# A hybrid decoder step on one core: order of loads, of shared-bank uses and of the opening MLP weights

## What is computed

```python
qa, ka, va, qb, kb, vb, fa = jnp.split(rmsnorm(x, g_attn) @ w_in, _SPLITS, axis=-1)
logf = jax.nn.log_sigmoid(fa + b_f)
s = jnp.einsum('bqhd,bkhd->bhqk', qa, ka) * scale + c_q - c_k          # forgetting: c = cumsum(logf), causal
oa = softmax(s) @ va
# dilated: for (w, d) in ((128, 1), (512, 4), (2048, 16)) a softmax over every d-th key of the last w; the three merged
x = x + concat(oa, ob) @ w_o
u = relu(rmsnorm(x, g_mlp) @ w_up)
y = x + (u * u) @ w_down
```

## Time and profile before

| | us |
|---|---|
| three timed runs | 3784.39, 3796.53, 3796.73 (median 3796.53) |
| the profiled execution, its own time | 3782.47 |
| span of its instructions | 3780.8 |
| projection / forgetting / dilated / samples (windows 0:691, 691:1167, 1167:1618, 1618:2010) | 691 / 476 / 451 / 392 |
| join, MLP of group 0 / of group 1 (2010:2144, 2144:2844 / 2844:2994, 2994:3781) | 134, 700 / 150, 787 |

### The profile page before, as it was taken

One profiled execution on the slowest core, in us unless ns is written; L12 is line 12 of the kernel. 1 busy time (PEld: TensorE's weight loads), 2 busy tenths in 40 slices (PEclk: granted clock), 3 DMA queues, 4 the chain that ended last, 5 costly groups with the idle time before them and its releaser, 6 DMA issues. The chain is left out here.

```text
span 3780.8 us, 50228 instructions
## 1 busy us (share of the span) xinstructions
PE 3532.7 (93%) x18196; PEld 2750.4 (73%) x18240; DVE 1486.2 (39%) x2869; ACT 981.8 (26%) x1424; POOL 1113.3 (29%) x1034
## 2 busy tenths in 40 slices
PE   7999999799998999979997899999998899999999
PEld 7987788455554777744445688888886788888888
DVE  2223323555535656243322343343333333333333
ACT  3322222244442222222222311112113311111111
POOL 1224366576665566501231200100101200000000
PEclk9999999899998999889998999999999999999999
DMA  6555766866657565388874211111104211111111
GB/s 199 189 172 187 229 198 222 208 158 184 182 142 191 151 179 173 109 316 310 299 257 158 67 50 45 44 44 55 55 31 154 59 45 44 37 42 39 39 44 62
DMA packets 303528, 507.60 MB, mean 134 GB/s; under 512 B 48850, under 2 KB 190676, under 8 KB 297940
## 3 DMA queue, kind: packets, MB, share of 16 engines
q1 hardware_dynamic: 266356, 370.29, 32.5%
q10 hardware_dynamic: 23032, 80.04, 6.2%
q0 software_dynamic: 13952, 54.80, 4.0%
HBM read 408.18 MB, written 164.50 MB: 151 GB/s over the span
## 5 line engine op out<-in xcount | busy, mean ns | idle before, releaser
L2900 DVE TENSOR_TENSOR fin_x<-mlp_y,fin_x 128x512 f32<-128x512 f32 x544 | 350.2, 686 | 749.8 <-PE mlp_y L2943 749.8
L2860 POOL TENSOR_TENSOR mlp_u<-fox_in_squares 128x1024 f32<-128x1024 f32 (+2 forms) x80 | 131.7, 1646 | 1325.2 <-ACT fox_in_squares L2801 1325.2
L2920 PE MATMUL mlp_u<-fin_h_hi,mlp_w_hi 128*128 128x512 f32 (+2 forms) x1280 | 451.0, 352 | 21.1 <-DVE mlp_w_lo L2876 21.1
L2921 PE MATMUL mlp_u<-fin_h_lo,mlp_w_hi 128*128 128x512 f32 (+2 forms) x1280 | 451.0, 352 | 0.0
L2922 PE MATMUL mlp_u<-fin_h_hi,mlp_w_lo 128*128 128x512 f32 (+2 forms) x1280 | 450.8, 352 | 0.0
L2943 PE MATMUL mlp_y<-mlp_w_hi,mlp_u_lo 128*128 128x512 f32 x1088 | 425.0, 391 | 0.0
L674 PE MATMUL proj_z<-proj_w_lo,proj_x_hi 128*128 128x512 f32 (+1 forms) x816 | 305.6, 375 | 0.0
L673 PE MATMUL proj_z<-proj_w_hi,proj_x_hi 128*128 128x512 f32 (+1 forms) x748 | 281.6, 376 | 11.8 <-DVE proj_w_lo L518 10.7
L675 PE MATMUL proj_z<-proj_w_hi,proj_x_lo 128*128 128x512 f32 (+1 forms) x748 | 276.2, 369 | 0.0
L2920 PEld LDWEIGHTS mlp_u<-fin_h_hi,mlp_w_hi 128*128 128x128 f32 x1280 | 241.5, 189 | 44.5 <-DVE mlp_w_lo L2876 21.7
L2921 PEld LDWEIGHTS mlp_u<-fin_h_lo,mlp_w_hi 128*128 128x128 f32 x1280 | 241.3, 188 | 22.2
(11 more groups left out here) (287 smaller groups left out, 6800.3 us busy)
## 6 DMA issues: line engine op xcount, KB each, us to landing
samp_v_in<-in_cache_v POOLq DMA_DIRECT2D x128, 256.0 KB, 4.8
fin_w_raw<-in_w_up SPq DMA_DIRECT2D x64, 512.0 KB, 3.8
fin_w_raw<-in_w_down SPq DMA_DIRECT2D x64, 512.0 KB, 3.9
out_new_win_k<-in_win_k ACTq DMA_DIRECT2D x8, 4080.0 KB
out_new_win_v<-in_win_v ACTq DMA_DIRECT2D x8, 4080.0 KB
samp_k_in<-in_cache_k SPq DMA_DIRECT2D x80, 256.0 KB, 4.7
proj_x_hi<-scratch_xt SPq DMA_DIRECT2D x34, 512.0 KB, 6.4
proj_x_lo<-scratch_xt SPq DMA_DIRECT2D x34, 512.0 KB, 6.4
```

Of the source, the lines that this page charges most:

```text
L2900: dve.tensor_tensor(part, y_ps[(tiles * par + t) % 2][0:rows, q * D_G:(q + 1) * D_G], part, ALU.add).then_inc(y_added, 1)
L2920: pe.matmul(out, hi, h_hi[:, k, c0:c0 + n], start=(k == 0), stop=False)
L2921: pe.matmul(out, hi, h_lo[:, k, c0:c0 + n], start=False, stop=False)
```

## The change

Six edits, all in the order of work; no product is added or left out. (1) In the projection's passes 1 and 2, SP issues the load of x before the store of the transposed rows. (2) In the forgetting attention, `turn_sums` follows the first quarter of a unit's low scores and `turn_back` the third; `turn_max` stands before `values`, `denominators` last; VectorE's list follows. (3) `values` runs in every unit, four products (eight instructions) a batch. (4) In the dilated attention, `turn_sums` stands between the two score groups, `turn_back` behind the second, `turn_max` before `values`, `denominators` last; low scores no longer precede the scores in the first step of a pair. (5) The first two tiles of the heads' output are loaded by SP in the sample stage, behind its last load of keys. (6) `w_hi` and `w_lo` are one pair of buffers for join and MLP; the first two weight pieces of the MLP are split at the end of the join; the low parts of the join's last two tiles go from GpSimd to VectorE.

```diff
@@ project, SyncE, passes 1 and 2
                     for j in range(2):
+                        load_xt(p, i, j + 2)
                         store_zt(p, i, j - 2)
-                        load_xt(p, i, j + 2)
                         store_z(p, i, j)
@@ attend_fox, VectorE
-                for todo in planned(G, "low"):
-                    largest(*todo)
-                for todo in planned(G, "turn"):
-                    take_off(*todo)
-                for n in ended(G - 3):
-                    invert(n)
-                for n in ended(G - 4):
-                    post(n)
+                todo = planned(G, "low")
+                for k in range(4):
+                    for x in todo[len(todo) * k // 4:len(todo) * (k + 1) // 4]:
+                        largest(*x)
+                    if k == 0:
+                        for n in ended(G - 3):
+                            invert(n)
+                    if k == 2:
+                        for n in ended(G - 4):
+                            post(n)
+                for x in planned(G, "turn"):
+                    take_off(*x)
@@ attend_fox, TensorE, in the loop over k (scores, low scores) and behind it
-                if G % 2 == 1:
-                    for x in (G - 2, G - 1):
-                        if 0 <= x < UNITS:
-                            values(x)
+                    if k == 0:
+                        for n in ended(G - 3):
+                            turn_sums(n)
+                    if k == 2:
+                        for n in ended(G - 4):
+                            turn_back(n)
+                for x in planned(G, "turn"):
+                    turn_max(*x)
+                if 0 < G <= UNITS:
+                    values(G - 1)
                 for n in ended(G - 2):
                     denominators(n)
-                for x in planned(G, "turn"):
-                    turn_max(*x)
-                for n in ended(G - 3):
-                    turn_sums(n)
-                for n in ended(G - 4):
-                    turn_back(n)
@@ attend_dilated, TensorE
-                first = len(todo) // 2 if G % NS_DIL == 0 and G > 0 else 0
-                for x in todo[:first]:
+                if G < STEPS:
+                    scores(G, 0)
+                for x in todo[:len(todo) // 2]:
                     low_scores(*x)
...
+                for n in macro_out(G, 1):
+                    turn_sums(n)
+                if G < STEPS:
+                    scores(G, 1)
+                for n in macro_out(G, 2):
+                    turn_back(n)
+                for x in todo[len(todo) // 2:]:
+                    low_scores(*x)
+                for x in planned(G, "turn"):
+                    turn_max(*x)
                 if 0 < G <= STEPS:
                     values(G - 1)
                 for n in macro_out(G, 0):
                     denominators(n)
...
@@ attend_samples, SyncE, behind the last load of keys
+            for t in range(2):
+                load_heads(sp, dram, o_in, o_loaded, P, 0, t)
@@ join_heads, SyncE
-            if g == 0:
-                load_o(0)
-            else:
+            if g == 1:
                 sp.wait_ge(sent, 16 * GROUPS_T[0][1])
...
-                if g == 0 and k == KC + 4:
-                    load_o(1)
@@ join_heads, ScalarE, before the last hi_h
+            act.wait_ge(product, 2 * tiles)
+            for q in range(2):
+                act.wait_ge(w_in["loaded"][q], 16)
+                act.activation(w_hi[:, q, :], w_in["raw"][:, q, :], ACT.Copy).then_inc(w_in["hi_done"], 1)
@@ join_heads, GpSimd
-                if t > 0:
+                if 0 < t < tiles - 1:
                     lo_h(t - 1)
-            lo_h(tiles - 1)
@@ join_heads, VectorE
-            gain(tiles - 1)
+            for t in (tiles - 2, tiles - 1):
+                if t == tiles - 1:
+                    gain(t)
+                n = rows_of[t]
+                dve.wait_ge(h_hi_done, t + 1)
+                dve.tensor_tensor(h_lo[:, :, t * P:t * P + n], hg[:, :].rearrange("p (k m) -> p k m", m=P)[:, :, 0:n],
+                                  h_hi[:, :, t * P:t * P + n].bitcast(F32), ALU.subtract).then_inc(h_lo_done, 1)
+                if t == tiles - 2:
+                    for q in range(2):
+                        dve.wait_ge(w_in["hi_done"], q + 1)
+                        dve.tensor_tensor(w_lo[:, q, :], w_in["raw"][:, q, :], w_hi[:, q, :].bitcast(F32),
+                                          ALU.subtract).then_inc(w_in["split"], 1)
@@ mlp, ScalarE hi_w and VectorE lo_w alike
-                for q in range(PIECES):
+                for q in range(2 if isinstance(b, int) and b == 0 else 0, PIECES):
```

More of the change, by code:

```diff
@@ L906, in x_uses @@
             for G in range(UNITS + 5):
-                for _n in ended(G - 2):
-                    use("den")
-                for _x in planned(G, "turn"):
-                    use("turn")
                 for _n in ended(G - 3):
@@ L914, in x_uses @@
                     use("back")
+                for _x in planned(G, "turn"):
+                    use("turn")
+                for _n in ended(G - 2):
+                    use("den")
             return uses
@@ L1482, in x_uses @@
             for G in range(STEPS + TAIL):
-                for _n in macro_out(G, 0):
-                    use("den")
-                for _t in planned(G, "turn"):
-                    use("set")
                 for _n in macro_out(G, 1):
@@ L1490, in x_uses @@
                     use("back")
+                for _t in planned(G, "turn"):
+                    use("set")
+                for _n in macro_out(G, 0):
+                    use("den")
             return uses
@@ L1846, in _ @@
                 todo = planned(G, "low")
-                first = len(todo) // 2 if G % NS_DIL == 0 and G > 0 else 0
-                for x in todo[:first]:
+                if G < STEPS:
+                    scores(G, 0)
+                for x in todo[:len(todo) // 2]:
                     low_scores(*x)
-                for z in range(2):
-                    if G < STEPS:
-                        scores(G, z)
-                    part = todo[first:]
-                    for x in part[len(part) * z // 2:len(part) * (z + 1) // 2]:
-                        low_scores(*x)
+                for n in macro_out(G, 1):
[4 more added lines that the diff above has]
+                    turn_back(n)
+                for x in todo[len(todo) // 2:]:
+                    low_scores(*x)
+                for x in planned(G, "turn"):
+                    turn_max(*x)
                 if 0 < G <= STEPS:
@@ L1859, in _ @@
                     denominators(n)
-                for x in planned(G, "turn"):
-                    turn_max(*x)
-                for n in macro_out(G, 1):
-                    turn_sums(n)
-                for n in macro_out(G, 2):
-                    turn_back(n)
 KV_SLOTS = 3
@@ L1950, in load_samp_in, with attend_samples @@
             .then_inc(samp_in["new_loaded"], 16)
[L1953 removed]
+def attend_samples(nc, c, dram, samp_in, spare, o_in, o_loaded):
     NUMBER, EMPTIED = turn_table()
@@ L2565, in _ @@
                 load_o(t)
-            load_mlp_in(sp, dram, w_raw_mlp, w_loaded_mlp)
+            load_mlp_in(sp, dram, w_in["raw"], w_in["loaded"])
         @block.scalar
@@ L2702, in _, with mlp @@
             turn_h(tiles - 1)
-def mlp(nc, c, dram, g, first, tiles, h_hi, h_lo, x1, w_raw, w_loaded, o_in, o_loaded, spare, out_sent):
+def mlp(nc, c, dram, g, first, tiles, h_hi, h_lo, x1, w_in, o_in, o_loaded, spare, out_sent):
     tokens = min(tiles * P, (TILES - first) * P + N_SAMPLE)
@@ L2720, in mlp @@
     with Phase(nc, f"mlp{g}") as ph:
-        w_hi = ph.sb("w_hi", [P, 2, PIECES, 1024], F32R)
-        w_lo = ph.sb("w_lo", [P, 2, PIECES, 1024], F32R)
+        w_raw, w_loaded, w_hi_done, w_split = w_in["raw"], w_in["loaded"], w_in["hi_done"], w_in["split"]
+        w_hi, w_lo = [w_in[x][:, :, :].rearrange("p (b q) f -> p b q f", q=PIECES) for x in ("hi", "lo")]
         r = spare[:, :].rearrange("p (f t) -> p f t", f=FB)
@@ L2981, with finish @@
 GROUPS_T = ((0, TILES // 2), (TILES // 2, TILES // 2 + 1))
-def finish(nc, c, dram, ph, o_in, spare):
+def finish(nc, c, dram, ph, o_in, o_loaded, spare):
     sent = ph.sem("out_sent")
-    o_loaded = [ph.sems(f"o_loaded{g}_") for g in range(2)]
     for g, (first, tiles) in enumerate(GROUPS_T):
-        w_loaded = ph.sems(f"w_loaded{g}_")
+        w_in = {"loaded": ph.sems(f"w_loaded{g}_"), "hi_done": ph.sem(f"w_hi_done{g}"), "split": ph.sem(f"w_split{g}")}
         with Phase(nc, f"fin{g}") as tile:
@@ L2994, in finish @@
             x1 = tile.sb("x1", [P, tiles, D_MODEL])
-            w_raw = tile.sb("w_raw", [P, 2, D_MODEL])
-            join_heads(nc, c, dram, g, first, tiles, h_hi, h_lo, x1, o_in, o_loaded[g], w_raw, w_loaded, sent)
-            mlp(nc, c, dram, g, first, tiles, h_hi, h_lo, x1, w_raw, w_loaded, o_in, o_loaded[1], spare, sent)
```

(5 more changed lines are left out.)

15 lines of the change are left out of this document (7 added, 8 removed).

## The result

The changed kernel takes 3770.89 us (median of 6 runs, 3761.84 to 3775.20) beside 3789.20 for the kernel before (6 runs, 3777.48 to 3796.73). The ratio is 0.9947, with a 95% interval of 0.9930 to 0.9963: faster by 18 us in the medians and 20 by the ratio, where 59 were forecast (3737 against 3796.53).

What follows compares the result with a forecast made beforehand. TensorE, busy 93% of the span, was taken as the bound, so only its idle or half-clock time pays. Terms of -18.4, -15.7, -8.1, -3.5 and -6.2 sum to -51.9: 3730.6, with 7 for the offset 3737 us; range 3704 to 3772.

Steps and rivals of the forecast that it cites:

- x ahead of the stores: Projection pass 1: loads no longer stand behind late stores, so waits for x go; -18.4 us, best -20.9, worst -10.
- forgetting: Forgetting attention: bank waits and stalls go, half clock returns, less batch borders and sums' copies; -15.7 us, from -29 to +2.
- dilated: Dilated attention: shared-bank waits mostly go, less new waits at `turn_back` and `turn_max`; -8.1 us, from -18 to +2.
- heads' output early, and opening weights: Joins and MLP starts: early first tiles give -3.5 us, opening weights split in the join -6.2 us.
- its 18.1: Dilated stage: waits for ScalarE's copies and VectorE's reads, 6.3 + 4.2 + 3.9 + 3.7 us; 15.1 expected gone.
- the 13.4: Projection pass 1: seven waits of TensorE for x, 13.4 us, expected to go with the load ahead of the store.
- The border's 8: Forgetting: 40 more P V batches at 0.2 us each for going in and out cost 8 us, between 0 and 16.
- The dips: Forgetting: five half-clock stretches behind `fox_qb` waits, 27.28 us, worth at most 13.6; 70% taken, 9.5 us.
- The clock at the batch borders: Rival: doubled small pauses in forgetting drop TensorE's clock; 3873 us if in each unit, 3805 one in two; chance 0.04.
- The second rival: Pass 1: x is issued earlier but other transfers hold its data, the waits stay; 3756 us; chance 0.10.
- The first rival: Forgetting and dilated: bank waits only move, both edits give nothing; 3754 us, with the offset 3761; chance 0.18.
- The 7 us for the offset: Whole kernel: half of the 14 us by which two of three timed runs exceeded the profiled execution, added to the sum.

Runs made afterwards that it cites:

- best: Changed kernel plus dilated store a step sooner, P V in batches of eight, later weight-piece split in pass 1, gates' loads first: 3709.11 us, ratio 0.9787 to before.
- send_early: Changed kernel, but ScalarE issues a dilated output's store in the step in which VectorE made it, not a step later: 3750.61 us, ratio 0.9889 to before.
- post_late: Changed kernel, but VectorE's `post` in the dilated stage stands behind the second half of the maxima: 3776.85 us, ratio 0.9953 to before.
- b_eights: Kernel before with forgetting's bank uses spread, but P V for two units in every second unit: 3755.13 us, ratio 0.9912 to before.
- a_alone: Kernel before with only the loads of x ahead of the stores: 3783.41 us against 3790.93, ratio 0.9988.
- lf_first: Changed kernel, with the gates' two small loads ahead of four masks in ScalarE's list in the sample stage: 3754.86 us, ratio 0.9908 to before.

## Why the prediction was wrong, step by step

The direction was right, the size was not: 59 us forecast, about 20 measured. Of the 59, 7 lay in the median of three runs (3796.53), which is 3789.20 with six. In stages, as means over the traces with and without each edit (best aside, and for the dilated stage also send_early and post_late, for the projection the two with the later split, for forgetting b_eights):

| part | forecast | measured |
|---|---|---|
| x ahead of the stores | -18.4 | -5.9 (675.0 to 669.1) |
| forgetting | -15.7 | -26.4 (487.8 to 461.3) |
| dilated | -8.1 | +16.5 (459.3 to 475.8) |
| heads' output early, and opening weights | -9.7 | -6.9 |
| sum | -51.9 | -22.7 |

The parts miss their forecasts by 12.5, -10.7, 24.6 and 2.8. That forgetting gave 10.7 more than forecast hides part of the other misses in the sum; this was luck.

**The dilated stage is the step that failed.** It was to give 8.1 and at worst to lose 2; it lost 16.5. The prediction looked for new waits of TensorE (`turn_back` on `invert`, `turn_max` on the maxima) and took VectorE's new order as free: the wait for a slot's store stands nowhere in its sum. It did not ask what is queued behind `post` when `post` waits for the slot of an older store. Moving `post` ahead of half the maxima put them behind a transfer, and putting the denominators last held ScalarE's store back by most of a step. The terms that it did price came in part: the four waits of its 18.1 fell to 9.6, and those for the reduced maxima rose by 5.1, where 5 was set aside for `turn_max`. But all waits for the bank together (`dil_x`) are 29.3 in both traces, and 23.4 with the store sooner. With the store sooner the stage takes 7.4 less than the mean of the unedited stage (459.3 to 451.9), close to the 8.1 forecast; but that is one trace beside seven that spread over 11 us, and the earlier store was not tried on the kernel before, so how much of it is the edit's is not shown. The ends given for the stage do not come out of its terms either: the best of them give -15.1 - 5.1 = -20.2 in place of -18, the worst -15.1 + 9 x 0.72 + 7 = -1.6 in place of +2.

**Pass 1 was put down to the wrong cause.** The row with SP's store at 311.22 was read rightly as late, and the prediction even named ScalarE's weight copy as the reason, but it then took the load's place in SP's list for the cause and priced the rest by when the rows were final in that one tile, 0.4 late. Measured were 0.8 to 1.7 in five tiles, and a last wait for x of 4.7 in the pair that the edit doesn't reach, since that pair's load stands in lines of its own behind its store. One of the seven waits of the 13.4 (0.87) lies in pass 2, which the prediction took to have none. ScalarE's waits, 92.0 us in that window of before, would have shown it.

**Forgetting** was forecast too low. Its idle time fell by 18.2, against 15.7 less the 1.5 for the sums: all five stalls at L1218 went, not four, and the sums' copies cost nothing (0.8 of waits for them, 2.9 before). Half clock fell from 44.2 to 13.4 us, worth 15.4, against 9.5. The border's 8 was right in its sum, though the half of it for coming out of a batch had no row behind it. The dips were priced by those behind the waits for `fox_qb` alone, 27.3 of the 44.2; the rest went as well, and that it stood behind other waits that went is likely but not shown.

**The opening weights** were right: 3.9 and 4.1 for 3.5 and 2.7. The early loads gave next to nothing, since the third tile took the wait over; 1 had been set aside for that.

**The rivals.** The clock at the batch borders did not fall: with a batch in every unit PEclk of the stage rose to 0.98. The Trainium skill ("TensorE: Matmul & The Clock Gate", section "A second HAM failure mode: psum-queue depth-cycling") tells of short pauses between groups of matmuls that make the clock swing; this stage has more borders than before, and its trace does not show it (13.4 us at half clock, 44.2 before). The second rival, transfers that hold the data of x, did not come: the waits for x fell from 13.4 to 4.7. The first rival, waits that only move, came true in the dilated stage, mostly by another mechanism than the one it named, and not in forgetting. The 7 us for the offset of the medians came true: 3789.20 is 6.7 above the profiled execution of before. That was one of the short ones, with 3.8 in a wait that takes 11.7 in a_alone.

## What to carry to other kernels

When an instruction is moved ahead of others on its engine, list everything it waits for, output slots and their stores included, and what now stands behind it; a wait that was harmless at the end of a list is not harmless in the middle. When a transfer is late because a store or load ahead of it in its queue waits, follow that wait to its first cause before the queue's order is changed: the waits of the engines off the critical path (here ScalarE's 92 us for a weight piece) name it. Compare stages over several traces before a few us are put down to an edit.

## What was not expected of the hardware

Small loads issued some 4 us into the samples' stage, with large loads around them, land in time in one trace and up to 12.9 us late in another, though that stage's own order of loads is the same; issued ahead of the masks, they were in time in both traces taken (lf_first and best), and the samples took 381.9 and 379.4. And in forgetting 18.2 us less idle time brought 30.8 us less at half clock (1.2 GHz), more than the forecast had; but half clock does not follow idle time everywhere: in the unedited dilated stage it is 64.4 to 99.2 us beside 44.1 to 47.4 us of idle time.
